# Score matmuls map by map, and value-projection ticks between the key-rotation drain ticks, in a one-core hybrid layer

## Time and profile before

| | us |
|---|---|
| median of three runs | 4300.85 (4298.69 to 4303.13) |
| span of the profiled execution, first to last instruction | 4303.9 |
| TensorE busy | 3099.8 (72%) |
| VectorE busy | 2705.5 (63%) |
| ScalarE busy | 1511.1 (35%) |
| moved by DMA | 1499 MB, 348 GB/s over the span |

### The profile page before, as it was taken

The page is one execution under the profiler, slowest core; times in us unless marked ns, Lnnn a source line. Parts: engine busy times, 40 slices in busy tenths (PEclk is TensorE's granted clock), DMA queues, the critical chain, the costliest instruction groups (busy, mean ns, idle before and its releaser), DMA issues. The chain is left out here.

```text
span 4303.9 us, 48708 instructions
## 1 busy us (share of the span) xinstructions
PE 3099.8 (72%) x15864; PEld 1982.7 (46%) x15864; DVE 2705.5 (63%) x7617; ACT 1511.1 (35%) x3085; POOL 1254.2 (29%) x1068
## 2 busy tenths in 40 slices
PE   6787798887788769778887679768776677733333
PEld 4676565665555337455554347444433254400000
DVE  1326357337667884477668873577678945776775
ACT  3533366312255651114555540223446611010010
POOL 0000111112233332333223332333334323355553
PEclk8888888898888779898888889888778788855555
DMA  7485767687989989998999899989999999999998
GB/s 261 157 305 189 278 243 267 254 319 307 357 343 375 360 309 390 404 415 354 363 362 366 351 359 384 417 344 402 375 372 386 363 410 415 398 408 415 416 406 336
DMA packets 269363, 1499.17 MB, mean 348 GB/s; under 512 B 44968, under 2 KB 81672, under 8 KB 97464
## 3 DMA queue, kind: packets, MB, share of 16 engines
q0 software_dynamic: 152064, 1107.36, 64.5%
q1 hardware_dynamic: 117048, 388.70, 24.0%
HBM read 1463.49 MB, written 31.36 MB: 347 GB/s over the span
## 5 line engine op out<-in xcount | busy, mean ns | idle before, releaser
L1698 POOL DMA_INDIRECT rt_ring<-in_peer_uv,rt_few_idx x1056 | 1250.9, 1185 | 3021.0 <-PE rt_acc L876 2385.5
L1644 DVE SCALAR_TENSOR_TENSOR rt_ring<-rt_ring,rt_h 128x1024 f32<-128x1024 f32 x1056 | 1265.9, 1220 | 504.7 <-DMA rt_ring<-in_peer_uv,rt_few_idx 481.7
L876 PE MATMUL rt_acc<-rt_ring,rt_diag 128*32 128x512 f32 x4224 | 759.9, 795 | 623.1 <-DVE rt_diag L1655 622.1
L625 PE MATMUL pair<-dense,w 128*128 128x256 f32 (+2 forms) x3056 | 598.6, 355 | 14.0 <-DMA w<-in_weights 12.2
L625 PEld LDWEIGHTS pair<-dense,w 128*128 128x128 f32 x3056 | 518.1, 199 | 128.8 <-issue 64.5
L614 PE MATMUL pair<-w,dense 128*128 128x256 f32 (+1 forms) x2352 | 556.4, 395 | 9.5 <-DVE dense L1300 3.5
L1199 ACT ACTIVATE rt_act_dot<-rt_dot 128x2 f32<-128x2 f32 x528 | 106.1, 202 | 1269.0 <-DVE rt_ring L1644 1262.1
L876 PEld LDWEIGHTS rt_acc<-rt_ring,rt_diag 128*32 128x32 f32 x4224 | 100.1, 122 | 953.4 <-DVE rt_diag L1655 810.1
L614 PEld LDWEIGHTS pair<-w,dense 128*128 128x128 f32 (+1 forms) x2352 | 436.2, 189 | 158.8 <-issue 72.9
L1655 DVE TENSOR_SCALAR rt_diag<-cst,rt_act_dot,rt_few_prob 128x32 f32<-128x32 f32 x1056 | 266.1, 296 | 119.9 <-ACT rt_act_dot L1199 109.5
L625 PE MATMUL bank<-dense,w 128*128 128x256 f32 (+2 forms) x1424 | 276.9, 351 | 1.7 <-DMA w<-in_weights 1.2
(11 more groups left out here) (241 smaller groups left out, 3248.5 us busy)
## 6 DMA issues: line engine op xcount, KB each, us to landing
w<-in_weights SPq DMA_DIRECT2D x284, 1024.0 KB
rt_ring<-in_peer_uv,rt_few_idx POOLq DMA_INDIRECT x1056
dense<-scratch_mod SPq DMA_DIRECT2D x18, 512.0 KB, 12.4
dense<-in_x_prompt SPq DMA_DIRECT2D x16, 512.0 KB, 13.5
rt_h<-scratch_h SPq DMA_DIRECT2D x33, 128.0 KB
rt_x<-scratch_x SPq DMA_DIRECT2D x132, 32.0 KB
out_k_prompt<-dense SPq DMA_DIRECT2D x32, 128.0 KB
out_v_prompt<-dense SPq DMA_DIRECT2D x32, 128.0 KB
```

Source lines behind the costliest of these rows:

```text
L625: mm = nc.tensor.matmul(bank[b][:, 0:n], wt[:, k * CH + j * P:k * CH + (j + 1) * P], src[:, k, 0:n], start=(k == 0), stop=(k == KC - 1))
L876: mm = nc.tensor.matmul(acc[u % 2][a * T:(a + 1) * T, :], diag[b % 2][:, i, :], slot[:, D + c * BANK:D + (c + 1) * BANK], start=(q == 0), ...
L1644: dt = nc.vector.scalar_tensor_tensor(up, up, 1.0, h2[u % 2][:], ALU.mult, ALU.mult, accum_out=dot[:, b % 2, i:i + 1])
L1698: nc.gpsimd.indirect_dma_start(ring[n % RING][:], None, d["peer_uv"], bass.IndirectOffsetOnAxis(ap=few_idx[u % 2][:, c:c + 1], axis=0)).th ...
```

## The change

Two edits. In `ticks` the dk drain ticks, which stood together ahead of the dv ticks, are set one after each of the first six dv ticks; all costs stay. In `attend` the loop over maps goes around the loop over chunks of 512 columns, and the wait for a map's exponential goes inside it. Before, both waits stood ahead of the first matmul, and the order was chunk 0 map 0, chunk 0 map 1, chunk 1 map 0, chunk 1 map 1.

```
     add("norm", nt + 2, 4.5)
-    for kind in ("dk", "dv"):
-        lag = 6 if kind == "dk" else 2
-        for i in range(4):
-            for ti in range(nt):
-                out.append(((kind, g, i * nt + ti), 3.6 if kind == "dk" else 3.0))
-        out.extend(((kind, g, 4 * nt + i), 1.0) for i in range(lag))
+    out.extend((("dk", g, i), 3.6) for i in range(4 * nt))
+    for i in range(max(4 * nt + 2, 6)):
+        if i < 4 * nt + 2:
+            out.append((("dv", g, i), 3.0 if i < 4 * nt else 1.0))
+        if i < 6:
+            out.append((("dk", g, 4 * nt + i), 1.0))
...
-                    for m in range(2):
-                        pe.wait_ge(at_exped[m], base + max(0, x if wide else x - 1))
                     o = BANK * (x % 2) if nk <= BANK else 0
...
-                    for c in range(0, nk, BANK):
-                        w = min(BANK, nk - c)
-                        for m in range(2):
-                            rows = slice(m * HD, (m + 1) * HD)
+                    for m in range(2):
+                        rows = slice(m * HD, (m + 1) * HD)
+                        pe.wait_ge(at_exped[m], base + max(0, x if wide else x - 1))
+                        for c in range(0, nk, BANK):
+                            w = min(BANK, nk - c)
                             mm = nc.tensor.matmul(pair[m][0:n, o + c:o + c + w], qd[rows, h, c0:c0 + n], keys_of[rows, c:c + w],
                                                   start=True, stop=True)
```

## The result

| | before, us | changed, us | ratio, 95% interval |
|---|---|---|---|
| first comparison, median of 4 runs each | 4301.99 (4298.69 to 4305.71) | 4267.77 (4260.76 to 4271.39) | 0.9913 [0.9899, 0.9928] |
| again, with the last experiments (6 against 17 runs) | 4302.76 | 4264.44 | 0.9908 [0.9887, 0.9929] |

The change makes the kernel 34 to 38 us faster (37 to 40 by the ratios). 4270 was forecast, with 4240 to 4290 as the range: right in sign and size. But of the two halves of the sum the drain's was a little too large and attention's too small by more than a factor of two.

What follows compares the result with a forecast made beforehand. Bounds by stretch: the engine chain before gathers, the trunk in group 1, full DMA in places, a three-engine loop with VectorE nearest full in attention. Gains 7.5 + 10 + 4 + 0 + 9 = 30.5 us gave 4270 us median, range 4240 to 4290.

Steps and rivals of the forecast that it cites:

- the drain: Key and value stages of all groups: dv ticks mixed with dk drain ticks fill TensorE's waits; 7.5 + 10 + 4 + 0 us.
- attention: Wide units of groups 2 to 4: earlier scores shorten VectorE's waits in 29 stalls; 9 us gained, bounds -8 and 30.
- Group 0: Key and value stage with nothing beside it: dv ticks fill TensorE's idle time; 7.5 us gained, bounds 4 and 10.
- Group 1: TensorE's 26.3 us wait before dots 0: dv ticks run inside it; 10 us gained, bounds 3 and 14.8.
- the step on late transfers: Group 1: value stores and weight loads go out late on SP beside first gathers, DMA full; 3.5 us taken off.
- D: Rival: late stores on SP give most of the drain back; gain 10 us, 4291 us, chance 0.15.
- Group 2: Rotation beside the next tile's selection: dv ticks fill TensorE's waits for VectorE; 4 us gained, bounds 0 and 8.
- Groups 3 and 4: Value stages before full DMA: TensorE's gain is spent waiting for gathers; 0 us, bounds -2 and 4 together.
- map 1's, whose first chunk is queued behind map 0's second chunk: Wide attention units: despite this queueing, map 1's maximum would start about 0.7 us earlier.
- TensorE ends such a unit up to 0.5 us later: Wide attention units at low clock: a cost set against the earlier start, leaving net 0.3 to 1.1 us per stall.
- B: Rival: attention gives nothing, VectorE's saved wait returns as another in the same tick; gain 21.5 us, 4279 us, chance 0.20.
- E: Rival, slower: map 1 runs only after both chunks of map 0, without overlap; 4319 us, chance 0.06.

Runs made afterwards that it cites:

- e10: Changed kernel with the transfers of unit 1 issued at step 5 instead of ahead of step 0; 4259.99 us, ratio 0.9898 to the kernel before.
- e9: Changed kernel with unit 1's transfers issued at step 5 and 22 instead of 14 ticks of group 1 in tile 0's selection; 4259.31 us, 0.9894 of before.
- e4: Kernel before with the matmuls map by map but both waits still ahead of the first; 4302.57 us, ratio 0.9997 to the kernel before.
- e2: Kernel before with the `attend` edit alone, `ticks` as before; 4280.84 us, ratio 0.9951 to the kernel before.
- e3: Kernel before, matmul order kept, each map's wait put ahead of that map's first matmul; 4284.34 us, ratio 0.9963 to the kernel before.
- e1: Kernel before with the `ticks` edit alone, attention as before; 4282.41 us, ratio 0.9958 to the kernel before.

## Why the prediction was right

**Group 0: mechanism right, size about right.** The steps came as worked out: store at 61.86 (61.4 said), wait of TensorE 3.05 us (2.1), end at 77.7 (76.5). 5.7 us reach the first gather, of 6.7 gained at the value stage; 7.5 was said. A single trace is loose here: step 0 came 1.0 to 8.5 us earlier than in the trace of before.

**Group 1: the step on late transfers was undersized.** Four dv ticks did go into the gap, 14.5 us of TensorE, yet 4.1 us came out; I had taken off 3.5 for full DMA and SP's queue, and it was 9 or more. Late value stores and loads hold ScalarE for 18.2 us (8.2 before) and TensorE for 3.6. D, as a mechanism, was right for this group alone. SP's place in the queue is the smaller part of it. ScalarE copies its first value tile out only at 444.1 us, after a wait of 23.6 us for the unit's `rt_h`. SP issues the store for it at 447.2, and the buffer comes free at 468.4, 21 us after the issue. In e10, where SP has nothing ahead of it, the store goes out at 445.9, right behind the copy, and the buffer still comes free only at 465.0. What these 3 to 4 us are worth at the end of the kernel e9 and e10 did not show.

**Group 2: right** (4 said, 4.5 found). Of the waits in the earlier trace rows the one of 5.0 us went.

**Groups 3 and 4: within the bounds, the mechanism not shown.** I said 0 and up to 4 for both, because a gain there would come back as a wait for gathers. The averages have 1.0 and 3.0, neither clear of 0 by its standard error of 1.4 and 2.2. The wait of 5.9 us in the earlier trace rows did go. That 5 to 6 us are gained in the stage and 3 to 4 given back behind it is what the rows by second gathers say, but for group 3 the rows by first gathers do not.

**Attention: the size was wrong, 9 said, 21.6 timed.** The step that failed is the order within TensorE: "map 1's, whose first chunk is queued behind map 0's second chunk", with "TensorE ends such a unit up to 0.5 us later". e4 shows that there is no such queueing, and the unit of the earlier trace rows and its fellow above end 4.17 and 4.06 us after the second exponential began. So nothing is paid for the earlier start.

The gain can be followed unit by unit. I took the 45 wide units that are not the first of their group, and in each the start of VectorE's maximum of map 1, counted from the start of the second exponential of the unit before. In e2 TensorE starts 0.9 us earlier and ends 0.1 us earlier (median), and the maximum comes 0.56 us earlier in the mean: 25 us in sum. The sum is 20 us in e3, 25 and 26 in the two traces of the changed kernel, and 0.5 and 1.5 in e1 and e4, where the wait is not split. That is the order of the timed gains: 21.6, 18, and nothing for e4. The gain of one unit differs. It is about 1.0 us in the unit above and little or nothing where VectorE is busy with other work when the scores arrive. My 9 us were 29 stalls at the low end of 0.3 us.

I took the low end because other waits of the loop would fill up, and they did not: VectorE waits 22 us less for the scores in the earlier trace rows, and its idle time in the three stretches fell by 23. DMA had the room: in group 2 it went from 308 to 325 GB/s, against 411 at the full rate. B is refuted by e2. E is refuted by e4: the loss of overlap that it needs does not exist, and its ground that TensorE's queue is in order does not hold between the two halves of the rows.

One part was overlooked. Of the 47 wide units 18 had their scores at a granted clock over 0.9 before and in e1 and e4, but 22 in e2, 24 in e3, and 24 and 26 in the two traces of the changed kernel. Ahead of the scores of all of them TensorE is idle for 102 us in sum in the first three and 62 to 63 in the others. How much of the gain is the clock's is not separated.

The Trainium skill (TensorEngine Tiling (Array Packing), Key Properties) says that tiles operate independently. I used it for neighbours in the queue alone. In e4 it holds for all four matmuls of a unit: 1.99 us in either order.

The total was near in part by luck. The drain came out 3 us under its 21.5 (group 1 alone 6 under, groups 3 and 4 together 4 over), attention 12 over its 9, and the sum 4 to 8 us over the forecast. The profiled executions shortened by more (45 and 51 us at the last step) than the timed runs did, which is why I go by medians for the whole and by averages over traces for the parts. Two readings were slightly off and change nothing: TensorE's idle time in group 0 is 6.30 + 2.53 = 8.8 us, not 8.6, and VectorE is busy for 88% of group 4's attention, not 86.

## What to carry to other kernels

Put a wait in front of the first instruction that needs it, not in front of the group: the reader of the first half (here VectorE's maximum) gains even if the writer ends hardly earlier (0.1 us here). Work moved into an idle gap pays only as far as its own transfers move with it; see what its stores and loads are queued behind. Where DMA is nearly full, part of what an engine saves can be lost again behind it (1.7 and 1.6 us behind attention here), and an edit that moves work between steps shifts the borders of its own stage. So measure such a gain at the end and not in its stage.

## What was not expected of the hardware

Matmuls on the two halves of TensorE's rows (64 partitions each) do not block one another in the queue: four of 512 columns take 1.99 us at the high clock (2.4 GHz, granted 1.00), in alternating order and in map-by-map order alike (e4). Near the low one (1.2 GHz, granted 0.53 and 0.55) they take 3.67 and 3.57. In e2 an instruction queued fifth started third.
